# One tile ahead of each feed-forward loop issues its products in another order

## What is computed

```python
def swiglu(x, w_gate, w_up, w_down):
    return (jax.nn.silu(x @ w_gate) * (x @ w_up)) @ w_down
...
    x = x + 0.5 * swiglu(rms_norm(x, ffn1_norm[l]), ffn1_gate[l], ffn1_up[l], ffn1_down[l])
...
    x = x + 0.5 * swiglu(rms_norm(x, ffn2_norm[l]), ffn2_gate[l], ffn2_up[l], ffn2_down[l])
```

## Time and profile before

| | us |
|---|---|
| median of 3 runs | 2566.87 |
| the three runs | 2564.77, 2566.87, 2596.13 |
| the profiled execution | 2564.79 |
| its span, first to last instruction | 2562.9 |
| TensorE busy (PE) | 2542.4 |
| weight loads busy (PEld) | 2199.8 |
| VectorE busy (DVE) | 1777.9 |
| ScalarE busy (ACT) | 1355.2 |

### The profile page before, as it was taken

The page is one execution under the profiler, slowest core; times in us unless marked ns, Lnnn a source line. Parts: engine busy times, 40 slices in busy tenths (PEclk is TensorE's granted clock), DMA queues, the critical chain, the costliest instruction groups (busy, mean ns, idle before and its releaser), DMA issues.

```text
span 2562.9 us, 39649 instructions
## 1 busy us (share of the span) xinstructions
PE 2542.4 (99%) x14144; PEld 2199.8 (86%) x14144; DVE 1777.9 (69%) x2715; ACT 1355.2 (53%) x2105; POOL 17.0 (1%) x20
## 2 busy tenths in 40 slices
PE   7999999999999999999999999999999999999999
PEld 6888888888888888888888887888888888888888
DVE  8787658777668666556676765778776665666655
ACT  6665565565566444444445545765544444444443
POOL 2000000000000000000000000000000000000000
PEclk9999999999999999999999999999999999999999
DMA  7554556454554554565555564444555555555554
GB/s 298 199 189 169 198 181 241 160 187 167 211 183 179 191 186 176 184 214 182 194 183 172 190 211 150 147 164 166 190 186 196 184 169 190 211 190 187 176 183 165
DMA packets 75532, 480.60 MB, mean 188 GB/s; under 512 B 8480, under 2 KB 11168, under 8 KB 31136
## 3 DMA queue, kind: packets, MB, share of 16 engines
q1 hardware_dynamic: 75424, 479.16, 53.2%
HBM read 475.72 MB, written 2.10 MB: 186 GB/s over the span
## 4 chain that ended last, share of the span: by engine, by line
PE 83%; DVE 1%; ACT 0%; issue 0%; ACTq 0%; DVEq 0%
PE acc L825 45%; PE acc L826 23%; PE acc L831 4%; PE acc L833 3%; PE acc L832 3%; PE score L825 1%; PE score L1100 1%; PE score L826 1%; PE head_ps L1123 0%; DVE low L1557 0%; PE turn_ps L1109 0%; PE head_ps L1124 0%; PE sums L1043 0%; ACT high L1179 0%; PE sums L1053 0%
## 5 line engine op out<-in xcount | busy, mean ns | idle before, releaser
L825 PE MATMUL acc<-xs,high 128*128 128x512 f32 x3968 | 1386.2, 395 | 3.4 <-DVE mix L1670 2.3
L1557 DVE TENSOR_TENSOR low<-raw,high 128x1024 fp32r<-128x1024 f32 (+2 forms) x972 | 1075.0, 1124 | 441.7 <-ACT high L1179 419.2
L1179 ACT ACTIVATE high<-raw 128x1024 fp32r<-128x1024 f32 (+2 forms) x972 | 942.3, 977 | 478.3 <-PE acc L826 348.4
L826 PE MATMUL acc<-xs,low 128*128 128x256 f32 x3968 | 1102.4, 278 | 0.0
L825 PEld LDWEIGHTS acc<-xs,high 128*128 128x128 f32 x3968 | 744.9, 188 | 177.9 <-DVE mix L1670 3.0
L826 PEld LDWEIGHTS acc<-xs,low 128*128 128x128 f32 x3968 | 746.6, 188 | 0.5
L825 PE MATMUL acc<-hidden,high 128*128 128x512 f32 x1408 | 488.3, 394 | 0.0
L1222 ACT ACTIVATE lowsum<-acc 128x256 f32<-128x256 f32 x345 | 132.4, 384 | 490.9 <-PE acc L826 489.8
L826 PE MATMUL acc<-hidden,low 128*128 128x256 f32 x1408 | 390.0, 277 | 0.0
L825 PEld LDWEIGHTS acc<-hidden,high 128*128 128x128 f32 x1408 | 264.0, 188 | 61.3
L826 PEld LDWEIGHTS acc<-hidden,low 128*128 128x128 f32 x1408 | 264.3, 188 | 0.0
(11 more groups left out here) (387 smaller groups left out, 2015.7 us busy)
## 6 DMA issues: line engine op xcount, KB each, us to landing
raw<-w_up_dram SPq DMA_DIRECT2D x176, 1024.0 KB, 4.8
raw<-w_down_dram SPq DMA_DIRECT2D x128, 704.0 KB, 4.1
raw<-w_in_dram SPq DMA_DIRECT2D x76, 1024.0 KB, 4.9
raw<-w_out_dram SPq DMA_DIRECT2D x32, 1024.0 KB, 4.8
raw<-w_heads_dram SPq DMA_DIRECT2D x24, 1024.0 KB, 4.8
raw<-w_mixout_dram SPq DMA_DIRECT2D x16, 1024.0 KB, 4.8
raw<-w_mem_dram SPq DMA_DIRECT2D x8, 1024.0 KB, 4.9
raw<-w_nat_dram SPq DMA_DIRECT2D x8, 1024.0 KB, 4.8
```

Source lines behind the costliest of these rows:

```text
L825: eng.matmul(bank_, hi, moving, start=start, stop=False)
L826: return eng.matmul(bank_[:, 0:S], lo, moving[:, 0:S], start=False, stop=stop)
L1179: eng.activation(high[:, s % SPLIT, to:to + n * P], raw[:, s % RAW, at_:at_ + n * P], ACT.Copy).then_inc((highs_a, highs_b)[piece], 1)
L1557: eng.tensor_tensor(low[:, s % SPLIT, w], raw[:, s % RAW, at_:at_ + n * P], high[:, s % SPLIT, w].bitcast(F32), ALU.subtract).then_inc((lo ...
```

## The change

The helper `product` is cut into its two halves. The last written-out tile ahead of the loop of `up10` and of `up20` gets a branch of its own: for blocks 0 to 7 it issues the eight long products, then the eight short ones; blocks 8 to 15 are issued as long and short in turn, as before. Waits and semaphore increments stay at the ends of the same pieces. All other tiles, the loops and the other engines are issued as before.

```diff
+            def product_high(bank_, hi, moving, start):
+
+                return eng.matmul(bank_, hi, moving, start=start, stop=False)
+
+            def product_low(bank_, lo, moving, stop):
+
+                return eng.matmul(bank_[:, 0:S], lo, moving[:, 0:S], start=False, stop=stop)
+
             def product(bank_, hi, lo, moving, start, stop):
 
-                eng.matmul(bank_, hi, moving, start=start, stop=False)
-                return eng.matmul(bank_[:, 0:S], lo, moving[:, 0:S], start=False, stop=stop)
+                product_high(bank_, hi, moving, start)
+                return product_low(bank_, lo, moving, stop)
...
+                elif r.name in ("up10", "up20") and i is None and k == r.first - 1:
+                    a = bank_free(k, 4)
+                    for first, end in ((0, 8),) + tuple((b, b + 1) for b in range(8, KT)):
+                        for b in range(first, end):
+                            if b % 8 == 0:
+                                piece_ready(b // 8)
+                            product_high(a, hl(b)[0], xs[:, b, :], b == 0)
+                        for b in range(first, end):
+                            last = product_low(a, hl(b)[1], xs[:, b, :], b == KT - 1)
+                            if b % 8 == 7:
+                                last.then_inc(products, 1)
                 elif r.kind == "tile":
```

## The result

| | before | changed |
|---|---|---|
| median, us (4 runs each) | 2566.59 | 2593.11 |
| all runs | 2564.77, 2566.30, 2566.87, 2596.13 | 2591.43, 2592.80, 2593.43, 2593.81 |
| span of the profiled execution | 2562.9 | 2591.9 |

The ratio of the times is 1.008, with a 95% interval of 1.0043 to 1.0117. The medians are 1.0% apart; the ratio is smaller because one of the four runs of before is at 2596. So the change costs less than the 2% that was set as the bound, but clearly something, and it is what rival B priced at 2593.

A forecast was written before the change was run, and what follows sets the result against it. The prediction took TensorE's one stream of products, with hardly any waits, as the bound; 2564.8 us profiled + 0 for moved products + 0 for cadence = 2564.8, given as 2566 to match a median, range 2562 to 2595.

The forecast's parts named there:

- rival B: Both feed-forward parts drop into the slower cadence behind the changed tiles, to their ends: 27.1 us more, 2593 us; chance 0.27.
- count of pairs behind the tiles: Pairs after the changed pieces: 1985 in `up10` and 2055 in `up20`, together 4040.
- The moved products: First term, sixteen products per changed tile: 2.774 us against 2.773, taken as zero; bounds -0.4 and +1.1 us for two tiles.
- cover: Second term: ScalarE's next slab split waits on the piece; second piece needs only `lows_b`; if uncovered, 0.54 us once per part.
- the third term: Cadence of the pair stream behind the changed pieces: zero if entered fast, 27.1 us for both parts if slower.
- A: The forecast: the stream behind the changed tiles goes on at 0.3467 us per pair, about 2566 us; chance 0.56.
- Rival C: Only one of the two feed-forward parts drops into the slower cadence: 2579 us; chance 0.11.
- D: The run lifts the stream behind the tiles to a pace faster than any in the trace: 108 us less, 2458 us; chance 0.03.
- E: A cadence worse than any held, 0.36 us at every pair behind the tiles: 54 us more, 2620 us; chance 0.03.

The follow-up runs named there:

- e2: The changed kernel's new order in tile 7 of `up10` alone, `up20` as before: six runs at 2577.7 to 2578.8 us, four at 2593.0 to 2595.8.
- e3: The changed kernel's new order in tile 3 of `up20` alone, `up10` as before: seven runs at 2577.6 to 2582.5 us, three at 2592.6 to 2594.2.
- e11: The changed kernel once more, no edit, beside the kernel before: seven runs at 2592.0 to 2595.3 us.
- e9: The changed kernel, with `mixout` tiles 2 to 14 each starting with eight and eight, then one of thirteen short groupings; no time given.
- e6: The changed kernel, with blocks 8 to 13 of the same tiles as three long, three short, twice: ten runs at 2592.7 to 2594.5 us.
- e10: The changed kernel's two tiles reordered as eight long, eight pairs, eight short: ten runs at 2565.3 to 2567.2 us, ratio 0.9962 to before.
- e13: As e10, but seven long, nine pairs, then the last seven short in the two tiles: seven runs at 2591.4 to 2593.5 us.
- e12: The order of e10 moved to earlier tiles of `in_a1`, `up10`, `mixout` and `up20`: twelve runs at 2565.9 to 2569.9 us, median 2568.44.

## Why the prediction was wrong

**What was right.** The bound (one stream of products, no wait), the two cadences and their sizes, and the count of pairs behind the tiles. Rival B's price was 27.1 us; the medians moved by 26.5, and the profiled pairs by 27.0. The moved products, costed at 0 with bounds of -0.21 and +0.54 per tile, cost 0.02 us in `up10` and 0.04 in `up20`. No cover was lost: the waits are as before. The Trainium skill's figure for back-to-back products ("TensorE: Matmul & The Clock Gate", section "Wait — 56ns, not 53.3ns?") gives an estimate of 2.60 us for the piece; the trace has 2.80.

**The step that failed** is the choice of the third term: "if the stream enters fast again, the term is zero", with 0.56 for it and 0.27 for B. I gave A the lead "because most entries end fast and both loops start from the fast cadence". Both reasons are void. Most entries followed other instructions than the changed tile, and the cadence on arrival doesn't count for eight and eight: in e2 the stream came in at 391 ns and left at 398, in e3 it came in slow and left the same. The term was 27.0 us, B's mechanism, in place of zero. The two rows that did resemble the new order, a run of long products and a run of short ones, both showed 0.36, and I argued them away, rows 7 on the ground that the pairs ahead were slow already. Eight and eight led to the slow cadence in all 12 instances that a profile shows with a pair directly behind (two in the result's profile, two in e11, one each in e2 and e3, and six in e9, four of which rest on the duration of one product). No timed run of the result, e2, e3 or e11 lies below the level that this asks for.

**The second fault** was to take one profile for the kernel. I read "both are in the fast cadence now" off one execution, though one of three times stood 31 us higher, and I had the price of that distance in hand. The runs since put only 57 of 108 of before on that level. The change takes away the chance of the two lower levels rather than adding a fixed 27 us. Against the mean of the 108 runs of before, 2573.7 us, it costs about 19.

**Rival C** (a different outcome in the two parts) is what before does by chance and what the changed kernel never did. D and E did not occur: no stretch read in the profiles is faster than 0.3467 or settles slower than 0.3534.

**What stays open.** Why TensorE has two cadences for one stream of instructions isn't shown; the rows read differ in starts and durations alone. Nor is it shown why eight and eight next to each other end slow. That a form takes a given state to a fixed next one rests on the 25 cases of three-three, and on e6, e10 and e13, each with one level in all its runs. What the states are inside the engine, and what first sets them apart from run to run, isn't shown; they were only seen through start times and durations.

## What to carry to other kernels

In a stream that TensorE alone bounds, read the distance from start to start in each long stretch, not only in one: two stretches of the same instructions that differ by 2% without a wait are a lever. Time a kernel often enough to see whether its times fall on levels before one profile is taken for it. Where they do, an order written out once ahead of a loop can pin the level for the whole loop, for better or worse. Here only runs told which, and the place counted as well as the order (e12); rows that show the very order that is put in weigh more than many rows of other orders.

## What the runs showed of the hardware

- A stream of long and short fp32r products with a weight load each, at the 2.4 GHz level throughout, has two stable paces, 0.3467 and 0.3533 us per pair, held over 2000 pairs, loop passes and slabs. The durations tell them: 391 or 392/394/395 ns against 395/398/403.
- A short interruption in the order of the products, without any wait, can switch the pace, in both directions. Eight long and eight short next to each other gave the slower one each time. Eight long, eight pairs, eight short in tiles 7 and 3 gave the faster in 10 of 10 runs; seven long, nine pairs, seven short the slower in 7 of 7.
- What a given interruption does depends on the phase in which the stream meets it. Three long, three short, twice, ended fast 17 times and slow 8 times, and each of the six states on arrival always led to the same end. Nine short products in a row ended fast behind a long product of 395 ns (4 of 4) and slow behind one of 403 ns (2 of 2).
- The same binary ran at 2566, 2580 and 2595 us on the same chip in one group of runs, by which of its parts happened to be in which pace.
